# A net in fp32 halves on TensorE: three seven-product chunks in 7 of its 13 wide rounds, and operand sums taken from the returning columns

## The reference

```python
D_MODEL, SEQ, D_FF = 2048, 256, 5632

def swiglu(h, w_in, w_out):
    gu = h @ w_in                                  # (256 x 2048) @ (2048 x 11264)
    gate, up = gu[..., :D_FF], gu[..., D_FF:]
    return (jax.nn.silu(gate) * up) @ w_out        # (256 x 5632) @ (5632 x 2048)

h = h + 0.5 * swiglu(rmsnorm(h, ffn1_norm[l]), ffn1_w_in[l], ffn1_w_out[l])
...
h = h + 0.5 * swiglu(rmsnorm(h, ffn2_norm[l]), ffn2_w_in[l], ffn2_w_out[l])
```

## Time and profile before

| | |
|---|---|
| median of 3 runs | 2669.44 us (2668.92 to 2669.6) |
| profiled execution, its own time | 2668.85 us |
| its span (first to last instruction) | 2667.1 us |
| PE busy | 2655.7 us (100%), 12038 matmuls |
| DVE busy | 1926.6 us (72%) |
| ACT busy | 1392.4 us (52%) |
| PE clock granted | full |
| DMA queue of SP, share of 16 engines | 63.4% |

### The profile page before, as it was taken

One profiled execution on the slowest core, in us unless ns is written; L12 is line 12 of the kernel. 1 busy time (PEld: TensorE's weight loads), 2 busy tenths in 40 slices (PEclk: granted clock), 3 DMA queues, 4 the chain that ended last, 5 costly groups with the idle time before them and its releaser, 6 DMA issues.

```text
span 2667.1 us, 32619 instructions
## 1 busy us (share of the span) xinstructions
PE 2655.7 (100%) x12038; PEld 2193.6 (82%) x12038; DVE 1926.6 (72%) x2464; ACT 1392.4 (52%) x1836; POOL 58.2 (2%) x64
## 2 busy tenths in 40 slices
PE   9999999999999999999999999999999999999999
PEld 7888888888888788888888888887888888888887
DVE  6888889886645466888888886758555576566566
ACT  6555555454544445555555454555554464675463
POOL 0000000000000000000000000030000000020000
PEclk9999999999999999999999999999999999999999
DMA  9767677677845466666576667755467576546754
GB/s 303 232 198 236 194 231 222 205 222 240 257 144 174 146 219 211 212 225 224 181 246 204 222 213 226 253 186 158 137 186 258 166 237 211 174 143 206 240 181 135
DMA packets 348575, 550.89 MB, mean 207 GB/s; under 512 B 40992, under 2 KB 120096, under 8 KB 347648
## 3 DMA queue, kind: packets, MB, share of 16 engines
q1 hardware_dynamic: 346624, 539.90, 63.4%
q0 software_dynamic: 1648, 8.86, 1.0%
q10 hardware_dynamic: 144, 0.04, 0.0%
HBM read 525.59 MB, written 23.07 MB: 206 GB/s over the span
## 4 chain that ended last, share of the span: by engine, by line
PE 98%; DMA 1%; SPq 0%; DVE 0%; ACT 0%; issue 0%; ACTq 0%; DVEq 0%
PE bank L1467 17%; PE bank L1469 17%; PE bank L1468 17%; PE bank L1536 14%; PE bank L1535 14%; PE bank L1534 14%; DMA raw<-in_ffn_w_in_dram 1%; PE bank L1426 1%; PE bank L1134 0%; PE bank L886 0%; PE bank L870 0%; PE bank L1114 0%; PE bank L568 0%; PE bank L840 0%; SPq L1315 0%
## 5 line engine op out<-in xcount | busy, mean ns | idle before, releaser
L1965 DVE TENSOR_TENSOR wlo<-raw,whi 128x1024 fp32r<-128x1024 f32 (+3 forms) x559 | 641.9, 1158 | 542.8 <-ACT whi L1616 537.8
L1616 ACT CAST whi<-raw 128x1024 fp32r<-128x1024 f32 (+3 forms) x559 | 548.9, 990 | 649.5 <-PE bank L1469 623.8
L1756 ACT CAST whi<-raw 128x1024 fp32r<-128x1024 f32 (+1 forms) x416 | 409.2, 998 | 413.3 <-PE bank L1536 405.8
L2125 DVE TENSOR_TENSOR wlo<-raw,whi 128x1024 fp32r<-128x1024 f32 (+1 forms) x416 | 463.3, 1150 | 67.3 <-ACT whi L1756 64.9
L1467 PE MATMUL bank<-whi,p_hi 128*128 128x512 f32 x1184 | 465.6, 393 | 3.1 <-DVE wlo L1965 3.1
L1469 PE MATMUL bank<-whi,p_lo 128*128 128x512 f32 x1184 | 461.1, 389 | 0.0
L1468 PE MATMUL bank<-wlo,p_hi 128*128 128x512 f32 x1184 | 460.9, 389 | 0.0
L1467 PE MATMUL bank<-whi,q_hi 128*128 128x512 f32 x864 | 340.6, 394 | 0.5 <-DVE wlo L1965 0.5
L1469 PE MATMUL bank<-whi,q_lo 128*128 128x512 f32 x864 | 336.6, 390 | 0.0
L1468 PE MATMUL bank<-wlo,q_hi 128*128 128x512 f32 x864 | 336.3, 389 | 0.0
L1467 PEld LDWEIGHTS bank<-whi,p_hi 128*128 128x128 f32 x1184 | 222.4, 188 | 52.7 <-issue 5.7
(11 more groups left out here) (381 smaller groups left out, 2984.6 us busy)
## 6 DMA issues: line engine op xcount, KB each, us to landing
raw<-in_ffn_w_in_dram SPq DMA_DIRECT2D x704, 256.0 KB, 3.8
raw<-in_ffn_w_out_dram SPq DMA_DIRECT2D x320, 256.0 KB, 4.0
raw<-in_w_in_a_dram SPq DMA_DIRECT2D x192, 256.0 KB, 3.1
raw<-in_w_in_mix_dram SPq DMA_DIRECT2D x128, 256.0 KB, 3.2
raw<-in_w_ple_gate_dram SPq DMA_DIRECT2D x128, 256.0 KB, 3.7
raw<-in_w_in_b_dram SPq DMA_DIRECT2D x128, 256.0 KB, 3.1
raw<-in_w_out_mix_dram SPq DMA_DIRECT2D x64, 256.0 KB, 3.3
raw<-in_w_o_a_dram SPq DMA_DIRECT2D x64, 256.0 KB, 3.7
```

Source lines behind the costliest of these rows:

```text
L1616: act.copy(whi[:, c % SPLIT, 0:n, 0:w], raw[:, c, 0:n, 0:w]).then_inc(hi_done, 1)
L1756: act.copy(whi[:, i % SPLIT, 0:n, :], raw[:, i % CH, 0:n, :]).then_inc(hi_done, 1)
L1965: dve.tensor_tensor(wlo[:, c % SPLIT, 0:n, 0:w], raw[:, c, 0:n, 0:w], whi[:, c % SPLIT, 0:n, 0:w].bitcast(F32), ALU.subtract).then_inc(lo_ ...
L2125: dve.tensor_tensor(wlo[:, i % SPLIT, 0:n, :], raw[:, i % CH, 0:n, :], whi[:, i % SPLIT, 0:n, :].bitcast(F32), ALU.subtract).then_inc(lo_d ...
```

## The change

`SEVEN` becomes `(1, 3, 5)`, and `seven(s, wide)` gives `(1, 5)` in the wide rounds of `in0` and `in1` other than round 0: 6 of the 13 rounds of a net have two seven-product chunks, 7 have three. The weight sums of chunk 1 are made in `begin_wide`, between the evacuations of the two blocks. Those of the other chunks come after the lo parts of their units, with the lo parts of the sums right behind them; ACT casts these sums after its cast of the first unit of the next chunk. DVE combines ahead of the lo part of unit 14. The operand sums of the `out` stages are made from `hidf` in chunk 5, behind the weight sums. `hidden_hi` and `hidden_lo` are one instruction each instead of two. A load into a slot of `raw` that was summed waits for the sum as well. The scratch for software DMAs is set to 8192.

```diff
-SEVEN = (2, 5)
+SEVEN = (1, 3, 5)
+SEVEN_TWO = (1, 5)
...
+        def seven(s, wide):
+
+            return SEVEN_TWO if s.name[4:] in ("_in0", "_in1") and wide else SEVEN
...
+        def early_halves(s, wide):
+
+            return ((s, 0), (s, 1)) if s.name[4:] == "_in0" and wide == 1 else ()
...
+        def hidden_operand(s, k):
+
+            if s.name[-1] == "2" or k not in (1, 3, 5):
+                return None
+            return by_name[s.name.replace("in", "out")], k // 2
...
                     for i in range(2 * CH):
                         sp.wait_ge(lo_done, unit_at(s, wide, i) + 1)
+                        if unit_at(s, wide, i) - CH in summed_units:
+                            sp.wait_ge(t24_sum, summed_units[unit_at(s, wide, i) - CH] + 1)
...
             def hidden_hi(s, k, u):
 
                 act.wait_ge(hid_moved[u], moved_by(s, k, u))
-                for j in range(2):
-                    ins = act.copy(pair_hi[s.hid_pair][:, k * 2 + j, :].rearrange("p (t q n) -> p t q n", t=TT, q=4),
-                                   hidf[:, u, :, j, :, :].rearrange("p q t n -> p t q n"))
-                ins.then_inc(hid_hi, 1)
+                act.copy(pair_hi[s.hid_pair][:, k * 2:k * 2 + 2, :].rearrange("p j (t q n) -> p (j t) q n", t=TT, q=4),
+                         hidf[:, u, :, :, :, :].rearrange("p q j t n -> p (j t) q n")).then_inc(hid_hi, 1)
...
             def wide_round(s, wide):
 
                 n = wides.index((s.name, wide))
+                sums_13_hi(s, wide, SEVEN[0])
+                sums_24_hi(s, wide, SEVEN[0])
                 for c in range(2, CH):
                     wide_hi(s, wide, 2 * c)
+                    if c - 1 in seven(s, wide)[1:]:
+                        sums_13_hi(s, wide, c - 1)
+                        sums_24_hi(s, wide, c - 1)
                     if c == CH - 1:
                         act.wait_ge(p_full, n + 1)
...
                         act.copy(parts_out[:, 0, :], bank[4][:, :]).then_inc(p1_out, 1)
                     wide_hi(s, wide, 2 * c + 1)
-                    if c in SEVEN:
-                        weight_sums_hi(s, wide, SEVEN.index(c))
-                    if c == 3:
-                        if s.kind == "ffn_out" and wide == 0:
-                            operand_sums_hi(s, 1)
-                        if s.kind == "ffn_in" and wide == 3:
-                            operand_sums_hi(after(s, 2 * wide)[0], 0)
+                    halves = early_halves(s, wide) + halves_behind(s, wide)
                     if c == 5:
-                        for s_, k_ in halves_behind(s, wide):
+                        for s_, k_ in halves:
                             hidden_hi(s_, k_, k_ % 2)
...
+                    if c == 6:
+                        for s_, k_ in halves:
+                            if hidden_operand(s_, k_):
+                                operand_sums_hi(*hidden_operand(s_, k_))
...
+            def hidden_sums(s, k):
+
+                back, i = hidden_operand(s, k)
+                whole = [sums_of["ffn_out"][0][:, i, m, :].rearrange("p (q n) -> p q n", q=4) for m in range(4)]
+                a11, a21, a12, a22 = (hidf[:, k % 2, :, j, t, :] for j in range(2) for t in range(TT))
+                dve.wait_ge(hid_hi, s.hid0 + k + 1)
+                dve.tensor_tensor(whole[2], a11, a21, ALU.subtract)
+                link(dve.tensor_tensor(whole[0], a22, a21, ALU.subtract))
+                link(dve.tensor_tensor(whole[1], whole[0], a11, ALU.add))
+                dve.tensor_tensor(whole[3], a12, whole[1], ALU.subtract).then_inc(op_sum, 1)
...
                 if before[2] is None:
                     evacuate(before[0], before[1], before[1] % 2)
+                    weight_sums(s, wide, SEVEN[0])
                 else:
-                    evacuate_wide(before[0], before[2])
+                    evacuate_wide(before[0], before[2], (0,))
+                    weight_sums(s, wide, SEVEN[0])
+                    evacuate_wide(before[0], before[2], (1,))
                 for i in range(2, 4):
                     wide_lo(s, wide, i)
 
             def wide_round(s, wide):
 
                 before = ahead_of(s, 2 * wide)
+                weight_sums_lo(s, wide, SEVEN[0])
                 for c in range(2, CH):
-                    if c in SEVEN:
-                        weight_sums(s, wide, c)
-                    wide_lo(s, wide, 2 * c)
                     if c == CH - 1:
                         combine_products(s, wide)
+                    wide_lo(s, wide, 2 * c)
                     wide_lo(s, wide, 2 * c + 1)
-                    if c in SEVEN:
-                        weight_sums_lo(s, wide, c)
                     if c == 2 and before[2] is not None:
                         finish_wide(before[0], before[2])
...
+                    if c in seven(s, wide):
+                        weight_sums(s, wide, c)
+                        weight_sums_lo(s, wide, c)
+                    halves = early_halves(s, wide) + halves_behind(s, wide)
+                    if c == 2 and s.name[4:] == "_in0" and wide == 2:
+                        operand_sums(s, 1)
+                    if c == 4 and s.name[4:] == "_in0" and wide == 2:
+                        operand_sums_lo(s, 1)
                     if c == 5:
-                        for s_, k_ in halves_behind(s, wide):
+                        for s_, k_ in halves:
+                            if hidden_operand(s_, k_):
+                                hidden_sums(s_, k_)
                             hidden_lo(s_, k_, k_ % 2)
...
+                    if c == 6:
+                        for s_, k_ in halves:
+                            if hidden_operand(s_, k_):
+                                operand_sums_lo(*hidden_operand(s_, k_))
```

More of the change, by code:

```diff
@@ L291, in ahead_of @@
             return flat[n - 1] if n else None
-        def seven_number(s, wide, i):
-            return 2 * wides.index((s.name, wide)) + i
+        def seven(s, wide):
+            return SEVEN_TWO if s.name[4:] in ("_in0", "_in1") and wide else SEVEN
+        seven_at = {}
+        for s, _, wide in flat:
+            if wide is not None:
+                for c in seven(s, wide):
+                    seven_at[s.name, wide, c] = len(seven_at)
         GAIN = dict(ffn1=0, mix=16, ffn2=32, final=48, pool=64, gla=72)
@@ L485, in unit_at, with split_tiles @@
             return (s.r0 + 2 * wide) * CH + i
+        summed_units = {unit_at(s, wide, 2 * c + n): seven_at[s.name, wide, c] for s, _, wide in flat if wide is not None
+                        for c in seven(s, wide) for n in range(2)}
         def unit_tiles(i):
             return (2 * (i // 2), 2 * (i // 2) + 1) if i % 2 == 0 else (2 * (i // 2) + 1, 2 * (i // 2))
-        def split_tiles(i):
-            return 1 if i % 2 and i // 2 in SEVEN else 2
+        def split_tiles(s, wide, i):
+            return 1 if i % 2 and i // 2 in seven(s, wide) else 2
         def operand_number(s, i):
-            return 6 * (s.name[3] == "2") + (i + 1 if s.kind == "ffn_in" else 3 + 2 * int(s.name[-1]) + i)
+            made = [("in", 0), ("in", 2), ("out0", 0), ("in", 1), ("out0", 1), ("out0", 2), ("out1", 0), ("out1", 1), ("out1", 2)]
+            return 9 * (s.name[3] == "2") + made.index((s.name[5:] if s.kind == "ffn_out" else "in", i)) + 1
+        def hidden_operand(s, k):
+            if s.name[-1] == "2" or k not in (1, 3, 5):
+                return None
+            return by_name[s.name.replace("in", "out")], k // 2
         def sums_done(eng, s, k):
@@ L1546, in seven_products @@
                     i = SEVEN.index(c)
-                    q = seven_number(s, wide, i)
-                    first, last_ = i == 0, i == len(SEVEN) - 1
+                    q = seven_at[s.name, wide, c]
+                    first, last_ = c == seven(s, wide)[0], c == seven(s, wide)[-1]
                     p1, p5, p7, p6 = (bank[b][:, :] for b in range(4, 8))
@@ L1803, in wide_round @@
                     wide_hi(s, wide, 2 * c + 1)
-                    if c in SEVEN:
-                        weight_sums_hi(s, wide, SEVEN.index(c))
-                    if c == 3:
-                        if s.kind == "ffn_out" and wide == 0:
-                            operand_sums_hi(s, 1)
-                        if s.kind == "ffn_in" and wide == 3:
-                            operand_sums_hi(after(s, 2 * wide)[0], 0)
+                    halves = early_halves(s, wide) + halves_behind(s, wide)
                     if c == 5:
-                        for s_, k_ in halves_behind(s, wide):
+                        for s_, k_ in halves:
                             hidden_hi(s_, k_, k_ % 2)
-                        if s.name[-3:] == "in0" and wide == 1:
-                            for k_ in range(2):
-                                hidden_hi(s, k_, k_)
+                    if c == 6:
+                        for s_, k_ in halves:
+                            if hidden_operand(s_, k_):
```

(27 more changed lines are left out.)

55 lines of the change are left out of this document (23 added, 32 removed).

## The result

| | before | after |
|---|---|---|
| median of 4 runs each, side by side | 2669.32 us (2668.92 to 2669.60) | 2692.41 us (2690.78 to 2697.09) |
| ratio, 95% interval | | 1.0089 (1.0072 to 1.0107) |
| profiled execution, its span | 2668.85, 2667.1 | 2697.09, 2695.3 |

The changed kernel is slower by 23.1 us (0.9%). 2689 was forecast. Its runs scatter over 6.3 us, those of before over 0.7.

The account below looks back on a forecast made before the run. PE, 100% busy with 98% of the chain, was taken as the bound. Saved matmuls (−9.5 us) and new waits summed to +19.8 us on 2668.85: 2689 us as a median, likeliest range 2680 to 2700, 8 in 10 2668 to 2707.

Parts of the forecast that it names:

- 42 matmuls: Fourteen more seven-product chunks each save PE three matmuls of 0.2267 us: −9.5 us.
- starts of rounds: Weight sums between the evacuations delay block 1: 0.05 us in each of 24 rounds following a wide one, +1.2 us.
- `in0` w1, chunk 1: Weight sums after a plain evacuation delay unit 2 by 1.23 us in both nets, angles 1.59 in the first: +4.1 us.
- `in0` w1, chunks 5 to 7: This round has its own halves, landed long ago, so the cast of unit 12 starts at its floor: 1.04 x 2, +2.1 us.
- ten rounds with operand sums: `in0` w2, w3 and `in1` w1 to w3, both nets: units 12 and 14 late, 1.32 us a round, +13.2 us.
- `out0` w0, `out1` w0: Four three-chunk rounds without operand sums, landing taken as 6.4 us: 1.74 us late in each, +7.0 us.
- `in2` w1: Same as the `out` rounds but with landing 5.5 us: 0.84 us in each of two rounds, +1.7 us.
- The mechanism: Chunk 5: unit 12's cast queues behind ACT's DMA wait; its lo part follows eight DVE instructions; 1.32 us in ten rounds.
- DVE gets there in time: Rival at unit 12: its lo part is ready in time, so the whole saving stands, 2660 us; chance 0.10.
- the clock falls: Rival: each wait in 18 rounds followed by 24 matmuls at 1.2 GHz, 98 us more, 2787 us; chance 0.02.
- H: Start of ACT's cast of unit 12, counted from E: 24.13 us, costing H − 22.81 in ten rounds with operand sums.
- E: Zero point of a wide round's timeline: when DVE sees the last unit of the round before used.

Follow-up runs that it names:

- Experiment 1: Changed kernel with ACT's casts of the weight sums of chunks 3 and 5 moved ahead of `hidden_hi`, right behind their own chunk's casts: 2668.70 us, ratio 1.0001.
- experiment 5: Changed kernel with the move of the returning columns issued on SP after the load of unit 13, not 15: 2679.73 us, ratio 1.0040.
- experiment 6: Changed kernel with five moves: sums' casts, first wide round's sums, angles, t2/t4 sums of chunk 1, and combination behind unit 14's lo part: 2660.59 us, ratio 0.9970.
- experiment 7: The kernel of experiment 6 with two seven-product chunks (1 and 5) in all 26 wide rounds: 2669.15 us, ratio 1.0002.
- experiment 4: The kernel of experiment 3 with `operand_sums_hi` moved behind ACT's cast of unit 14: 2696.14 us, ratio 1.0103.
- experiment 3: Changed kernel with the operand sums and their half's `hidden_lo` moved behind the lo parts of units 12 and 13: 2711.19 us, ratio 1.0160.

## Why the prediction was right, term by term

The forecast was 2689 us and the median is 2692.4, slower by 23.1 us where 19.8 was the sum. Measured terms are how late PE's matmuls start beyond their spacing, summed over the rounds of the changed kernel's profiled execution.

| term | forecast | measured |
|---|---|---|
| 42 matmuls | −9.5 | −9.5 |
| starts of rounds | +1.2 | +2.3 |
| `in0` w1, chunk 1 | +4.1 | +3.9 |
| `in0` w1, chunks 5 to 7 | +2.1 | +2.0 |
| ten rounds with operand sums | +13.2 | +18.3 |
| `out0` w0, `out1` w0 | +7.0 | +7.0 |
| `in2` w1 | +1.7 | +2.4 |
| outside the wide rounds | 0 | +1.4 |
| sum | +19.8 | +27.8 (span: 28.2) |

- **The mechanism held**: a wait for a DMA, with the casts of unit 12 and of the sums behind it, then eight instructions of DVE. Experiment 1 took the casts of the sums out of the queue and experiment 5 took the late landing; the first gave back 23.7 us, the second 12.7 (medians). None of the rivals in which DVE gets there in time, or the clock falls, came about in the changed kernel. Late weights are no cause either: no cast of weights in a wide round waits for its load.
- **Mis-sized: H in the ten rounds with operand sums.** This is the step that failed in the sum. H was 24.17 to 25.63, 24.90 on average, instead of 24.13. The landing was not at fault: I took 5.6 us, and it took 4.61 to 6.07, 5.62 on average; in the same ten rounds of the kernel before it took 5.57, and the median of all there is 5.5. The 5.88 of the round shown above is on the slow side. Two other terms of H were too small. The move was issued at E + 18.01 on average, 0.54 later than the 17.47 of the prediction: six rounds lie at 17.43 to 17.65, but four at 18.31 to 19.23. In each of these four one single issue, of the 14 that SP makes from the start of the store to the move, took 1.12 to 2.02 us instead of the usual 0.43 or so. Two of them:

```profile
1353.68 1.57 SPq L1288 DMA_DIRECT2D hidden_squares<-hidq  x1
...
1443.90 2.02 SPq L1370 DMA_DIRECT2D raw<-in_ffn_w_in_dram  x1
```

  What makes an issue long is not shown. And the cast of unit 12 started 1.27 us behind the first landing, not 1.06, since the second half round lands 0.7 later on average and its cast waits for it. Some 0.15 of the average costs nothing, as the whole round starts late.
- **Mis-sized: the starts.** Not 0.05 in 24 rounds, but about 0.2 in the 12 that follow a round whose unit 14 was late, and next to nothing in the others. On DVE four lo parts still stand between the combination and the evacuation of block 0, so the delay is carried on. I had started every round from an undisturbed one. In experiment 6, where nothing is late at unit 14, it is gone.
- **Not foreseen**: 1.4 us outside the wide rounds, of which 0.7 is a wait for `q_lo` in `out2` of the first net. It is missing in the two kernels with two seven-product chunks in `in2` w1 (before and experiment 7) and 0.3 to 1.1 us in the others. In experiment 6 it goes back to the store and the returning DMA; what sets its size I didn't try, so that stays open.
- **Right by measurement**: the saving per matmul (9.5 in the wide rounds of experiments 6 and 7), chunk 1 of `in0` w1, and `out0` w0 and `out1` w0 (H 25.13 to 25.61, 25.16 forecast). In `in2` w1 the sum is near and the two nets are not: 2.0 in one and 0.4 in the other, 0.84 forecast for each. That they come near 1.7 together is luck.
- The profiled execution was the slowest of the four. Its 28 us stand beside 23 of the median; the four lie 21.5 to 27.8 us above the median of before. So the median shows an error of 3 us in the sum, and the table, which shows 8, is that of the slowest execution. That the others had earlier issues or landings is likely, but they were not traced.
- One thing stays open at the edge: experiment 4 lies 3.7 us above the changed kernel by the medians and 2.4 below it by the spans of the profiles. With intervals that overlap (1.0089 to 1.0117, 1.0072 to 1.0107), no difference is shown.

## What to carry to other kernels

For each instruction that waits for a DMA, list what stands behind it in the same engine's order. Then time the whole way to it, not the landing alone: here the landing was as taken, and what came late was the issue, and the second of two transfers behind the first. A busy share of 52% (ACT) or 74% (DVE) says nothing on this: two casts moved past a wait for a DMA and one for PE changed 1% of the time with no work added or removed. Saved matmuls count only where the engine that prepares their operands reaches the next unit in time, and when an instruction is moved, check both what stands behind it and who waits for its result on another engine; experiment 3 missed the second.

## What the runs showed of the hardware

- **The clock after a wait.** In experiment 3 PE's matmuls came late by 2.1, 2.35, 2.5 and twice 2.7 us in five rounds, and one to seven matmuls after the restart the spacing rose to 0.42 or 0.43 us, the lower of the two levels (1.2 GHz), for some seven or eight matmuls, about 1.5 us each time. Behind two more of 2.7 us, in the second net, it did not; nor behind any of 1.9 or less, there or in experiment 4, nor in the changed kernel, where the longest in a wide round was 1.7. So the length of the stop alone doesn't decide it, and what does is not shown.
- **The price of a restart.** In the wide rounds the first matmul behind a wait lasts 0.47 to 0.50 instead of 0.39 us (0.80 at the lower clock above) and the next starts 0.31 to 0.34 after it, not 0.23, in every version that has such waits. That is about 0.1 us for each wait, and it comes behind one of 0.16 us as well as behind one of 1.5.
- **The returning DMA** took 3.6 to 6.6 us from issue to landing in the wide rounds of the changed kernel, for the same 256 KB, and up to 7.4 before. Issued two loads earlier, it took 3.2 to 5.8. Two such DMAs issued 0.47 us apart landed about 0.7 apart in the ten rounds.
- **Issues on SP's queue** follow each other about 0.47 us apart in the round shown, so that the 14 from the start of the store to the move are the 6.66 us between them. Of the 2280 in the changed kernel the median lasts 0.43 us, 52 last over 1.0 and the longest 2.02.
